# Moving one chunk's scores into the stage before it, and sharing a final normalization between three engines, in a hybrid decoder step

## The reference

```
x_n = RMSNorm(x)
[u | v | r, k, v_b, low-rank columns | gate_A | gate_B] = x_n @ W_in
A = u * causal spatial gating of LayerNorm(v), chunks of 128
B = RWKV-7 recurrence on 16 heads of 64:
    s = s * w_t + (s a_t) b_t^T + v_t k_t^T ;  y_t = s r_t
x = x + W_o(sigmoid(gate_A) * (A @ P_A) + sigmoid(gate_B) * (B @ P_B))
x = x + MoE(RMSNorm(x))          (32 experts, two per token)
y = RMSNorm_final(x)
```

## Time and profile before

| | us |
|---|---|
| median of 3 runs | 1181.93 (1179.15 to 1182.7) |
| the profiled execution | 1178.33 |
| its span from the first to the last instruction | 1176.2 |
| PE busy in it | 1077.2 (92%) |
| DVE, ACT, POOL busy | 486.1, 288.4, 211.5 |
| mean granted PE clock | 0.98 of full |

### The profile page before, as it was taken

The page is one execution under the profiler, slowest core; times in us unless marked ns, Lnnn a source line. Parts: engine busy times, 40 slices in busy tenths (PEclk is TensorE's granted clock), DMA queues, the critical chain, the costliest instruction groups (busy, mean ns, idle before and its releaser), DMA issues. The chain is left out here.

```text
span 1176.2 us, 25289 instructions
## 1 busy us (share of the span) xinstructions
PE 1077.2 (92%) x10717; PEld 827.6 (70%) x10717; DVE 486.1 (41%) x1152; ACT 288.4 (25%) x585; POOL 211.5 (18%) x269
## 2 busy tenths in 40 slices
PE   5999999799999999999999999999995999986874
PEld 5888888688888887888777888886453555543541
DVE  4455555565565635555456201001454422211126
ACT  3243224345544441000254110000111211111102
POOL 4001000144553500000000058000001222212120
PEclk9999999899999999999999999999996999999997
DMA  8032222020000003229312222900977899999975
GB/s 243 1 104 65 56 56 57 23 56 4 4 4 4 4 13 103 59 72 234 95 37 72 68 76 55 269 35 23 408 286 276 336 416 415 414 417 416 417 316 218
DMA packets 114049, 183.08 MB, mean 156 GB/s; under 512 B 10369, under 2 KB 88733, under 8 KB 105242
## 3 DMA queue, kind: packets, MB, share of 16 engines
q1 hardware_dynamic: 107293, 168.59, 41.2%
q0 software_dynamic: 5168, 8.56, 2.0%
q10 hardware_dynamic: 1485, 4.39, 1.0%
HBM read 173.24 MB, written 17.55 MB: 162 GB/s over the span
## 5 line engine op out<-in xcount | busy, mean ns | idle before, releaser
L192 PE MATMUL rk_ps<-xT,rk_w 128*128 128x260 f32 x768 | 172.6, 385 | 0.0
L192 PEld LDWEIGHTS rk_ps<-xT,rk_w 128*128 128x128 f32 x768 | 144.6, 190 | 26.9 <-issue 2.7
L192 PE MATMUL psv<-xT,w_merge 128*128 128x260 f32 x480 | 107.7, 383 | 0.0
L192 PEld LDWEIGHTS psv<-xT,w_merge 128*128 128x128 f32 x480 | 91.1, 190 | 13.9
L2141 DVE SCALAR_TENSOR_TENSOR ex_sg<-tl_psA,ex_slot_rs,ex_sg 128x128 f32<-128x128 f32 x32 | 11.2, 351 | 139.7 <-ACT ex_sg L1941 139.5
L1414 POOL TENSOR_TENSOR spare<-spare,sv 128x4096 f32<-128x4096 f32 x1 | 8.9, 8855 | 277.6 <-DVE r_all L1383 277.6
L192 PE MATMUL uv_psu<-xT,w_uv 128*128 128x260 f32 x256 | 57.5, 383 | 1.2 <-ACTq L1084 1.2
L192 PE MATMUL mg_psp<-ya,w_merge 128*128 128x260 f32 x256 | 57.6, 383 | 0.0
L192 PE MATMUL psv<-xT,w_uv 128*128 128x260 f32 x256 | 57.4, 382 | 0.0
L192 PE MATMUL mg_psp<-r_all,w_merge 128*128 128x260 f32 x256 | 57.4, 382 | 0.0
L192 PEld LDWEIGHTS uv_psu<-xT,w_uv 128*128 128x128 f32 x256 | 48.0, 190 | 8.8 <-ACTq L1084 1.7
(11 more groups left out here) (497 smaller groups left out, 2007.2 us busy)
## 6 DMA issues: line engine op xcount, KB each, us to landing
wd<-in_moe_w_down SPq DMA_DIRECT2D x15, 1024.0 KB
rk_w<-in_w_in SPq DMA_DIRECT2D x24, 512.0 KB, 6.2
tl_x<-in_moe_w_down SPq DMA_DIRECT2D x9, 1024.0 KB, 20.3
w_uv<-in_w_in SPq DMA_DIRECT2D x16, 512.0 KB, 5.4
w_merge<-in_w_in SPq DMA_DIRECT2D x16, 512.0 KB, 4.3
xT<-in_moe_w_gate SPq DMA_DIRECT2D x5, 1024.0 KB, 20.1
xT<-in_moe_w_up SPq DMA_DIRECT2D x5, 1024.0 KB, 23.6
bonus_all<-in_moe_w_gate SPq DMA_DIRECT2D x5, 1024.0 KB, 19.8
```

Of the source, the lines that this page charges most:

```text
L192: last = eng.matmul(out[:, h, 0:TH], weights[:, k, :], xT[:, k, h * TH:(h + 1) * TH], start=(k == 0), stop=(k == NK - 1))
```

## The change

Five edits, in two places far apart and one at the start.

1. SP loads the sample rows before the prompt tiles; ACT squares them first; both inverse roots of the first part wait for one more square.
2. Two PSUM tensors, `m.psv` and the new `m.ps1`, are opened before `phase_inputs` and used in both phases. Behind the r/k/v loop PE makes the first chunk's scores of pairs 0 to 3 into `m.psv` and of pairs 4 to 6 into `m.ps1`. The last pair's scores come first in `phase_chunks`.
3. `turn_bk_v(0, 0)` is put ahead of the turning of the sample rows, and ACT's copy of its result ahead of the copy of the sample rows.
4. In the final stage PE also adds up the sample rows, into `psC` (six matmuls behind `kept`, in front of `combined`), with a small diagonal `diag_s` that DVE makes (two instructions).
5. DVE takes two roots there, `root(0, 3)` and `root(3, 5)`, not three. For the sample rows and tiles 0 and 2 DVE only multiplies by the gain (`gained`, ahead of the root), and ACT scales by the root (`scaled_act`, behind it). Tiles 1 and 3 stay with DVE's `scaled`.

```diff
+def pair_scores(eng, m, banks, pair):
+    n, lo, hi = pair % GP, slice(0, HD), slice(HD, P)
+    one, other = (b[:, n * P:(n + 1) * P] for b in banks)
+    for rows, which in ((lo, 0), (hi, 1)):
+        eng.matmul(one[rows, :], m.bk[rows, pair, rows], m.L[rows, pair, which, :], start=True, stop=True)
+    for rows, others, which in ((lo, hi, 0), (hi, lo, 1)):
+        last = eng.matmul(other[others, :], m.bk[rows, pair, others], m.L[rows, pair, which, :], start=True, stop=True)
+    return last
...
-        psp = [ps(f"rk_ps{n}", [P, 2, 512]) for n in range(2)]
+        psp = [m.psv, ps("rk_ps1", [P, 2, 512])]
-        pss = ps("rk_pss", [P, 2, 512])
+        pss = m.ps1
...
+            eng.dma_start(x_tile[NT], a["x_sample"][:, 0, :]).then_inc(s_x[NT], 16)
             for j in range(NT):
                 eng.dma_start(x_tile[j], a["x_prompt"][0, j * P:(j + 1) * P, :]).then_inc(s_x[j], 16)
-            eng.dma_start(x_tile[NT], a["x_sample"][:, 0, :]).then_inc(s_x[NT], 16)
...
+            eng.wait_ge(s_cols, 3 * NP + 1)
+            eng.wait_ge(s_first, 8 * GP)
+            for pair in range(GP):
+                last = pair_scores(eng, m, (m.psv[:, 0], m.psv[:, 1]), pair)
+            last.then_inc(m.s_scored, 1)
+            eng.wait_ge(s_ss_read, NP + 1)
+            eng.wait_ge(s_first, 8 * (NP - 1))
+            for pair in range(GP, NP - 1):
+                last = pair_scores(eng, m, (m.ps1[:, 0], m.ps1[:, 1]), pair)
+            last.then_inc(m.s_scored, 1)
...
-            for j in range(NT + 1):
+            for i, j in enumerate((NT, 0, 1, 2, 3)):
...
-                eng.wait_ge(s_sq, last)
+                eng.wait_ge(s_sq, NT + 1 if first else last + 1)
...
+            pair_scores(eng, m, bank[1][0:2], NP - 1).then_inc(s_eo[1], 1)
             for n in range(3):
                 last = eng.transpose(bank[1][2][0:3 * NSH, n * P:(n + 1) * P],
                                      m.shift_last[:, 3 * n:3 * n + 3, :].rearrange("p t c -> p (t c)"), m.ident[:, :])
             last.then_inc(s_sh, 1)
-            scores(0, 0)
-            scores(0, 1)
+            turn_bk_v(0, 0)
             eng.wait_ge(s_lw, 6)
...
                 for g in range(G):
-                    turn_bk_v(c, g)
+                    if c or g:
+                        turn_bk_v(c, g)
...
+            def scored(c, g):
+                if c == 0:
+                    eng.wait_ge(m.s_scored, g + 1)
+                if c or g:
+                    eng.wait_ge(s_eo[g], c + g)
...
+            eng.wait_ge(s_fy[NT], 16)
+            for h in range(2):
+                at_h = slice(h * 512, (h + 1) * 512)
+                eng.matmul(psC[0:TS, h, :], m.ident[0:TS, 0:TS], fxs[:, at_h], start=True, stop=False, skip_group_check=True)
+                for c in range(2):
+                    last = eng.matmul(psC[0:TS, h, :], diag_s[:, c, :], fys[0:TS, c, at_h], start=False, stop=(c == 1),
+                                      skip_group_check=True)
+            last.then_inc(s_fps, 1)
             combined(psA, 0)
             combined(psT, 2)
...
+            def scaled_act(i, dst):
+                n = size[final[i]]
+                eng.activation(dst, dst, ACT.Copy, scale=rstd[0:n, i:i + 1]).then_inc(s_fo_act, 1)
...
             square_final(3, flat(psT[:, :, :]), P)
-            eng.wait_ge(s_fs, 3)
+            eng.wait_ge(s_froot, 1)
+            eng.wait_ge(s_fm, 2)
+            scaled_act(0, fxs)
+            scaled_act(1, fx[:, 0, :])
+            eng.wait_ge(s_fs, 2)
             eng.wait_ge(s_fsq, 3)
             square_final(4, fx[:, 3, :], P)
+            eng.wait_ge(s_froot, 2)
+            eng.wait_ge(s_fm, 3)
+            scaled_act(3, fx[:, 2, :])
...
-            sum_up(NT)
-            root(0, 1)
+            def gained(src, dst, gain):
+                eng.tensor_tensor(dst, src, gain, ALU.mult).then_inc(s_fm, 1)
+
+            eng.wait_ge(s_fps, 1)
+            eng.wait_ge(s_fsq, 1)
+            gained(psC[0:TS, :, :], by_half(fxs), by_half(gf[0:TS, :]))
             sum_up(1)
-            scaled(0, fxs, fxs, gf[0:TS, :])
-            root(1, 3)
+            eng.wait_ge(s_fp, 1)
+            eng.wait_ge(s_fsq, 2)
+            gained(psA[:, :, :], by_half(fx[:, 0, :]), by_half(gf[:, :]))
+            root(0, 3)
+            eng.sem_inc(s_froot, 1)
             sum_up(3)
-            scaled(1, psA[:, :, :], by_half(fx[:, 0, :]), by_half(gf[:, :]))
+            eng.wait_ge(s_fp, 2)
+            eng.wait_ge(s_fsq, 4)
+            gained(psT[:, :, :], by_half(fx[:, 2, :]), by_half(gf[:, :]))
             scaled(2, fx[:, 1, :], fx[:, 1, :], gf[:, :])
             root(3, 5)
-            scaled(3, psT[:, :, :], by_half(fx[:, 2, :]), by_half(gf[:, :]))
+            eng.sem_inc(s_froot, 1)
             scaled(4, fx[:, 3, :], fx[:, 3, :], gf[:, :])
```

More of the change, by code:

```diff
@@ L249, in phase_inputs @@
         s_scaled_late = sem("t_scaled_late")
-        s_pi, s_ex, s_norm_used, s_first = (sem("f_" + n) for n in ("pi", "ex", "norm_used", "first"))
+        s_pi, s_ex, s_norm_used, s_first, s_last = (sem("f_" + n) for n in ("pi", "ex", "norm_used", "first", "last"))
         turn_order = (0, 1, NT, 2, 3)
@@ L665, in scores @@
                 b = bank[g]
[L666 to L677, removed]
+                eng.wait_ge(s_ar, c * 4)
+                eng.wait_ge(s_bk, c * 4)
+                eng.wait_ge(s_rh_e[g], 2 * c)
+                eng.wait_ge(s_w_e[g], c * NL)
+                for p in range(g * GP, (g + 1) * GP):
+                    last = pair_scores(eng, m, b[0:2], p)
                 last.then_inc(s_eo[g], 1)
@@ L825, in _, with first_z @@
                .then_inc(s_sv_e, 1)
-            for c in range(NC):
+            def first_z(c):
                 for g in range(G):
@@ L829, in _, with turned @@
                     eng.activation(Z[:, grp(g), :], b64(bank[g][0]), ACT.Copy).then_inc(s_z1[g], 1)
-                for g in range(G):
-                    if c:
+            def turned(c, g):
+                b = bank[g]
+                eng.wait_ge(s_tb[g], c + 1)
+                eng.activation(bkt[:, grp(g), :], b4(b[2]), ACT.Copy).then_inc(s_bkt[g], 1)
+                if g == 1:
+                    eng.activation(wv[hi, grp(g), 0, :], b64(b[3])[hi], ACT.Copy).then_inc(s_v_e[g], 1)
+                    eng.activation(wv[lo, grp(g), 1, :], b64(b[3])[lo], ACT.Copy).then_inc(s_v_e[g], 1)
+            eng.wait_ge(s_zero, 2)
+            for c in range(NC):
+                first_z(c)
+                if c:
+                    for g in range(G):
                         eng.wait_ge(s_st[g], c)
@@ L1539, in phase_tail @@
         s_fy = [sem(f"f_y{j}") for j in range(NTT)]
+        s_fps, s_fm, s_fo_act, s_froot = (sem("f_" + n) for n in ("ps", "m", "o_act", "root"))
         s_fx, s_diag, s_fp, s_fs, s_fsq, s_fo, s_out = \
@@ L1606, in _ @@
                 eng.dma_start(fy[j // 2][:, j % 2, :, :], rows[j * P:(j + 1) * P]).then_inc(s_fy[j], 16)
-            for i, j in enumerate(final):
-                eng.wait_ge(s_fo, i + 1)
-                if j < NT:
-                    eng.dma_start(a["y_prompt"][0, j * P:(j + 1) * P, :], fx[:, j, :]).then_inc(s_out, 16)
-                else:
-                    eng.dma_start(a["y_sample"][:, 0, :], fxs).then_inc(s_out, 16)
+            eng.wait_ge(s_fo_act, 1)
+            eng.dma_start(a["y_sample"][:, 0, :], fxs).then_inc(s_out, 16)
+            for j, (done, n) in ((0, (s_fo_act, 2)), (1, (s_fo, 1)), (2, (s_fo_act, 3)), (3, (s_fo, 2))):
+                eng.wait_ge(done, n)
+                eng.dma_start(a["y_prompt"][0, j * P:(j + 1) * P, :], fx[:, j, :]).then_inc(s_out, 16)
             eng.wait_ge(s_out, 16 * NTT)
@@ L2230, in _ @@
                     step.did(eng.tensor_scalar(diag[:, d, c, :], m.ident[:, :], m.weight[:, c, at[j]:at[j] + 1], None, ALU.mult))
+            for c in range(2):
+                step.did(eng.tensor_scalar(diag_s[:, c, :], m.ident[0:TS, 0:TS], m.weight[0:TS, c, at[NT]:at[NT] + 1], None, ALU.mult))
             step.wait()
```

36 lines of the change are left out of this document (19 added, 17 removed).

## The result

The changed kernel takes 1185.78 us (median of 20 runs, 1182.17 to 1188.91), against 1178.75 (1176.63 to 1184.97) for the kernel before on the same chip: a ratio of 1.0049, 95% interval 1.0038 to 1.0060. It is slower, by about 5.8 us by the ratio (the two medians alone lie 7.0 apart); forecast was −2.4, counted from the median of three runs, 1181.93. The profiled execution took 1185.49 with a span of 1183.4, where before had 1178.33 and 1176.2.

What follows compares the result with a forecast made beforehand. It took the chunk loop as bound by PE and the later expert phase by DMA. Chunk phase −2.9, start +0.2 and final stage +0.3 gave −2.4, from 1181.93 to 1179.5 us; range 1177.0 to 1182.3.

Steps and rivals of the forecast that it cites:

- six matmuls at 3.70 / 8 each end at 1154.8: Final stage: PE's six sample-row matmuls, begun when `kept` ends at 1151.98, are done at 1154.8.
- the forecast's 0.5: Final stage: `root(0, 3)` starts at 1160.9, 0.5 later than `root(1, 3)` did at 1160.40.
- Slower: Rival: the clock stays at half through the final stage's sums, including the sample rows; +5.8, 1187.7; chance 0.05.
- Its price of 0.43 for each matmul: Final stage, in rival "Slower": each sample matmul at half clock adds 0.43 to DVE's start.
- six of them eat the gain: Final stage, in rival "Slower": six sample matmuls at half clock, 0.43 each, use up the gain; from there the sign turns.
- What is won in front of the chunk loop should reach the end whole: Ahead of the chunk loop: time won there, taken as 2.9, arrives undiminished at the kernel's end.
- from there on the order is unchanged, so the gain is: Chunk phase from `turn_bk_v(0, 1)` on: gain 2.7 by PE's list, 3.3 by POOL's; 2.9 taken.
- It comes 0.3 later: End of final stage: both stores come together, 2.62 for both; the earlier sets the end, 0.3 later.
- the prediction's three signs of being wrong: First level does not move, PE's idle time between the turns grows, or the final stores do not overlap.
- the second root, forecast +0.45: Final stage: the second root at span-relative +0.45, 1170.1 where it was 1169.65.
- The start: Edit 1, sample rows loaded first: nothing won, up to 0.5 lost; +0.2 taken.
- the edit does nothing: Rival: barrier or memsets move back by what is won, so the end stays at 1182; chance 0.06.

Runs made afterwards that it cites:

- the final edits alone: Only edits 4 and 5 (final stage) put into the kernel before: 1182.62 us against 1179.43, ratio 1.0029.
- the pad: 48 (in some kernels 24) matmuls of eight columns, adding to no output, in PE's idle time before the barrier; 48 with the chunk edits: 0.9993 and 0.9971.
- the loads spread: Edits 2 and 3 in the kernel before, with the four w_uv loads issued one by one in chunks 0 to 3: 1180.53 us, ratio 1.0010.
- the three parts alone: Three kernels, each the kernel before with one part: edits 4 and 5 1.0029, edits 2 and 3 0.9996, edit 1 1.0002.
- the pad alone: The kernel before with only the small matmuls added in PE's idle time, 48 (run twice) or 24: 1.0009, 0.9990 and 0.9990.
- the final edits on 128 rows: Edits 4 and 5 in the kernel before, the six sample matmuls done on 128 rows of other data: ratio 1.0021.
- chunk edits: Only edits 2 and 3 (scores moved, turns reordered) put into the kernel before: 1180.03 us, ratio 0.9996.

## Why the prediction was wrong

**The step that failed most: "six matmuls at 3.70 / 8 each end at 1154.8".** The 3.70 us of the earlier trace rows are eight PE instructions, but only four `matmul` calls (two halves by two choices). I divided by instructions and multiplied by calls. Six calls are twelve instructions; they took 5.3 us at full clock (1155.91 to 1161.22), and 6.78 in the changed kernel, where the clock fell. The term of 2.8 was thus short by 2.5. The root came 4.75 later than before by the common mark, not 0.5. With the matmuls at full clock it came 3.2 later (15.70 against 12.52), which is about the forecast's 0.5 and the 2.5 that were missing; the other 1.6 go with the clock. In time: with the six matmuls the change is at 1.0049, without them at 1.0006, and with the final edits alone it is 1.0029 against 1.0003. So this step, with the fall of the clock that came with it, is worth 3 to 5 us. In the changed kernel's trace the two instructions of one call take 0.86 at full clock (1152.85 to 1153.71), 0.43 each, which makes 5.2 for the six calls.

**The rival of the slower side was near, and its chance too small.** "Slower" had the right place and the right sign: sums of the sample rows, the clock at half in part of them. Its price of 0.43 for each matmul was for the clock; the same 0.43 was owed at full clock for the second instruction of every call. Its condition, "six of them eat the gain", was met without it. It got 0.05. That its total, +5.8, is also what the ratio gives is luck: it put 8.5 on the final stage and won 2.7 elsewhere, where the traces have 4.8 in the final stage and nothing won at the end of the chunk loop.

**"What is won in front of the chunk loop should reach the end whole" failed.** The mechanism up to the first level was right and its size good: forecast 2.9, shown 3.0 to 3.2 behind the head sums in every kernel with these edits. DVE's mask (231.41, forecast 231.8), POOL's product (233.05, forecast 233.3) and `turn_bk_v(0, 1)` (236.74, forecast 237.0 to 237.6) came as said. But "from there on the order is unchanged, so the gain is" took PE's order for its only limit. The loop also waits for instructions, and where it starts earlier it waits more: PE now comes to the place where the next packet of its instructions starts while the loads of `w_uv` are running at some 290 GB/s, the packet starts 2.4 to 2.5 us late, and 2.4 to 2.6 us of waits follow at once. The rows were there: the waits of PE had "issue" with 7 us in sum, which the prediction left out, and the earlier trace rows had 4 GB/s in a stretch with hardly a load, which it did not ask about. That the waits grow by most of what was won is shown with and without the pad, and that the loads make the first of them by the one trace with the loads spread. Why the waits with the pad grow too (2.3), and why the spread did not bring the gain to the end, stays open. These waits are 3 to 6% of the loop's time (5.0 to 10.7 of some 190 us).

**The stores were right.** "It comes 0.3 later" was the sum of 0.75 kept from DVE and 1.05 for two stores that come together. From DVE's last instruction to the end of the span it is 1183.4 − 1178.28 = 5.1, where before had 1176.2 − 1172.13 = 4.1: +1.0. With the sample sum on DVE and the clock full, the last DVE instruction is 23.1 behind the mark, 1.1 earlier than before: forecast 0.75. So the two roots and ACT's scaling are worth nothing in the end because they bring the last two stores together. None of the prediction's three signs of being wrong came: the first level moved, PE's idle time between the turns shrank, the stores overlapped. The sign that spoke was the second root, forecast +0.45 and found 4.8 later behind the mark (24.41 against 19.59).

**The start was not contradicted** (+0.2 is too little to measure), and the discarded rival "the edit does nothing" was not what happened either.

**What is chance here.** Of the profiled 7.2 us, 2.5 lie between the chunk loop and the final stage, where nothing was changed. The clock was at half for longer there (0.94 against 0.97 in the mean of 1027 to 1136), and this part took from 712.3 to 721.0 us in the eighteen traces, with the same code in it (713.4 before, 715.9 in the changed kernel). In the whole kernels' medians it does not appear: the three parts alone give 0.29 + 0.02 − 0.04 = 0.27%, the whole change 0.49% with an interval down to 0.38%; what lies between is inside the intervals of the parts.

**What stays open.** Why the pad shortens the loop by some 4 us, of which the waits for instructions account for 1.3 and 2.3 and PE's busy time between the first level and `w_uv` for another 1.2 (178.0 against 179.2 in the mean, for the same 5831 instructions). Whether the pad alone shortens the time: three runs gave 1.0009, 0.9990 and 0.9990, though their traces are 3 to 5 us ahead at the first `w_uv` matmul; the stretch behind it, which varies by more than that, can hide it.

## What to carry to other kernels

Price an instruction by a row that holds the same call: count how many instructions one call makes before dividing or multiplying. Before giving a gain in front of a long unrolled loop to the end, look at what that loop waits for beside its operands. Waits for nothing that the profile shows, each 2.2 to 2.95 us behind the start of a 16 KB packet of the instruction queue, took this gain back; look whether large loads run where such a packet is due. And when one engine's work is moved to another to start it earlier, follow the first instruction behind it: here every root, product and store stood behind the moved sum.

## What the runs showed of the hardware

A float32 matmul of 512 columns was two PE instructions of 0.43 us at a granted clock of 1.00, with weights of 8 by 8 (1.88 us for four at 1153.71 in the changed kernel) as with weights of 128 by 128 (1.88 for four at 1156.77 in the final edits on 128 rows). In the chunk loop PE's waits for instructions ended 2.2 to 2.95 us behind the start of a 16 KB packet in all kernels (216 waits in eighteen traces), and 47 to 49 of the packets started between 222 and 434, one in 4.3 to 4.5 us in the mean. A packet started when PE had come to a certain place of its list (2448 to 2453 matmuls and weight loads in four of the five kernels without chunk edits and pad), and 2.4 to 2.5 us later than that in the three traces in which 290 GB/s of loads were running at that place. The granted clock fell to 0.50 while PE ran narrow matmuls without a pause (from 1156.5 on in the changed kernel, 0.58 in the mean of 1156.00 to 1159.60), and in six other traces in, or within 0.4 us behind, PE's idle time ahead of `combined(psA)` (3.62 us with the final edits and the sum on DVE).
